# What is kept of the input projection: added by VectorE at every further visit instead of brought back to PSUM

## The chip, the cores and the metric

The program runs on one core of a Trainium2 chip. The metric is the device time of the whole program in microseconds (us); less is better. The engines named here are TensorE (PE, matmuls; PEld is its weight load), VectorE (DVE), ScalarE (ACT), GpSimd (POOL) and SyncE (SP, which issues the loads). Matmul results go to PSUM, which here is used in banks of 128 x 512 fp32.

## What is computed

Two residual layers over 256 tokens of width 2048. Only the first projection of the first layer matters for the change:

```
mod = (silu(c) @ ada_w[layer] + ada_b[layer])
sh_m, sc_m, g_m, sh_f, sc_f, g_f = split(mod, 6)
h = rmsnorm(x, norm_mix[layer]) * (1 + sc_m) + sh_m
z = h @ w_in                       # (256, 2048) @ (2048, 5632)
q, k, v, u, vg = split(z)          # 12 heads, 4 gating groups
...                                # rope(q), rope(k), attention, spatial gating, w_out, residual, FFN
```

Everything is fp32. Each weight matrix is used as a high part (fp32r) and a rest (fp32r), and so is `h`, so that one product takes three matmuls: high x high, high x low, low x high.

## The kernel before, in words

**Weights.** All weights are streamed in pieces of 128 x 1024 fp32 (512 KB), 8 slots deep (`raw`). ScalarE copies a piece to its high part (`hi_piece`, L557), VectorE subtracts it from the piece to get the rest (`lo_piece`, L902), in the same slot. Here both are called splits. Two pieces make a unit: 24 matmuls of 128 x 512 (L1345 to L1347), 12 for each half of the tokens (t = 0, 1). Every engine walks the same list of units: in its turn n it prepares the pieces of unit n+2, while TensorE works through the unit that it has reached. What an engine does within a turn is in order; turns of different engines are tied by semaphores alone.

**The projection's order.** The 11 column groups of `w_in` (512 columns each) need 16 row tiles of 128, in four quarters of `h`. The quarters of `h` become known late, since each needs a part of the modulation `mod`. So the groups are visited more than once. `VISITS` lists them: visits 0 to 10 take quarter 0 of all 11 groups, visits 11 to 28 take one more quarter each of the first six groups (18 visits of one unit), and visits 29 to 33 take three quarters at once of the other five. Visit v of 0 to 28 is unit v. Visit v accumulates in PSUM banks `acc_bank(v, t)`, which it shares with visit v-2; `freed` waits for the visit before to be out of a bank.

**What happens between visits.** After a first visit ScalarE copies the two banks to `kept` or `vtok` in SBUF (`evict`, L585). For the 18 visits in `SEEDED`, ScalarE copies what is kept back to PSUM ahead of the visit (`seed`, L591), TensorE waits for it (`begin`) and accumulates onto it with no start flag, and ScalarE copies the sum out again. For visits 29 to 33 VectorE adds PSUM to what is kept, in place (`add_visit`, L1136). In a turn n of VectorE this stands between the two splits; in a turn of ScalarE the copies stand around its second split.

**The modulation.** `ada_w` is streamed too, in the same SP queue. VectorE sums it row tile by row tile: one operation of 128 x 1024 for each (`ada_op`, L930), 16 for one result, at a pace written out by hand in `ADA_PACE`: turns 9 to 20 have 32 of them (2 or 3 a turn), turns 21 to 59 have 66 (1 or 2 a turn). They stand at the end of VectorE's turn. In `REDUCE_AT` (turns 9, 15, 21) TensorE, after its unit, turns two tiles of the normalized x and then reduces the finished result over the partitions (`reduce_cols`, L1395, 16 records). It waits for the last sum, which stands at the end of VectorE's turn 8, 14 and 20. VectorE then adds the bias (`keep_cols`, L948), and ScalarE and VectorE make the next quarter of `h`. SP issues the load of sum number a only after sum a-6 is done, and the pieces that follow it in the queue wait with it.

**After it.** GpSimd applies rope to q and k after the last visit of a group (`whole`), from turn 23 on. Turns 28 to 46 hold the attention, whose scores VectorE reads at the head of its turn.

Of the kernel before, what the change touches and what calls it, by code (L numbers as in the profile page):

```python
# [53 lines left out]
VISITS = ([(c, (0,)) for c in IN_ORDER]  # L54
          + [(c, (k,)) for k in (1, 2, 3) for c in IN_ORDER[:EARLY]]
          + [(c, (1, 2, 3)) for c in IN_ORDER[EARLY:]])
# [3 lines left out]
VISIT_AT = {u: v for v, u in UNIT_OF.items()}  # L60
BEFORE = {v: w for v, (c, ks) in enumerate(VISITS) for w in range(v) if VISITS[w][0] == c}

SEEDED = [v for v in BEFORE if len(VISITS[v][1]) == 1]
KEPT = {c: n for n, c in enumerate((0, 3, 1, 4, 2, 5, 9, 10))}
FIRST_OF = {k: min(u for u, x in enumerate(IN_UNITS) if x[2] == k) for k in range(4)}

# [10 lines left out]
G_F0 = G_OUT + 4  # L77
SEEDED += [G_F0 + n for n in range(2 * F_VISITED, len(F_UNITS))]
G_CI = G_F0 + 30 + 6 * F_VISITED
# [154 lines left out]
def acc_bank(g, t):  # L234
    return 2 * (g % 2) + t
# [6 lines left out]
def decoder_kernel(nc, x_in, c_col, pos, ada_w, ada_b, g_mix, g_ffn, w_in, sgu_w, sgu_b, w_out,  # L242
                   conv_in, conv_w, conv_out, ff_gate, ff_up, ff_down, g_fin, freq_in, ident_in,
                   mask_in, out):
    with ExitStack() as ctx:
# [148 lines left out]
        def kept_of(c, t):  # L394
            return kept[:, KEPT[c], t, :] if c in KEPT else vtok[:, t, COLS * (c - 6):COLS * (c - 5)]
# [156 lines left out]
        def _(sa):  # L552
# [30 lines left out]
            def evict(dst, g, t, func=ACT.Copy):  # L583
                sa.wait_ge(acc_done[t], g + 1)
                nc.scalar.activation(dst, ps[:, acc_bank(g, t), :], func).then_inc(acc_free[acc_bank(g, t)], 1)  # L585

            def seed(src, g, t, before):

                freed(sa, before, t)
                freed(sa, g - 2, t)  # L590
                nc.scalar.activation(ps[:, acc_bank(g, t), :], src, ACT.Copy).then_inc(seeded, 1)  # L591
# [62 lines left out]
            def keep_visit(v, t):  # L654

                if v not in BEFORE or v in SEEDED:
                    evict(kept_of(VISITS[v][0], t), v, t)
                if v + 2 < G_OUT and v + 2 in SEEDED:
                    seed(kept_of(VISITS[v + 2][0], t), v + 2, t, BEFORE[v + 2])
# [239 lines left out]
        def _(ve):  # L899
# [5 lines left out]
            def lo_next(u, half):  # L905
                if half:
                    row_low_part(u)
                if 2 * (u + 2) + half < PIECES:
                    lo_piece(2 * (u + 2) + half)
# [220 lines left out]
            def add_visit(v):  # L1130

                for t in range(2):
                    of = kept_of(VISITS[v][0], t)
                    ve.wait_ge(acc_done[t], v + 1)
                    freed(ve, BEFORE[v], t)
                    nc.vector.tensor_tensor(of, ps[:, acc_bank(v, t), :], of, ALU.add).then_inc(acc_free[acc_bank(v, t)], 1)  # L1136
# [40 lines left out]
            for n in range(46):  # L1177
# [16 lines left out]
                lo_next(n, 0)  # L1194
                if VISIT_AT.get(n) in BEFORE and VISIT_AT[n] not in SEEDED:
                    add_visit(VISIT_AT[n])
# [135 lines left out]
        def _(pe):  # L1332
            def half_unit(u, g, t, first, last, of, k0, half):

                v = 2 * u + half
                on = g in SEEDED
                to = ps[:, acc_bank(g, t), :]
# [15 lines left out]
            def begin(g, t):  # L1353
                if g in SEEDED:
                    pe.wait_ge(seeded, 2 * SEEDED.index(g) + t + 1)
                elif g >= 2:
                    freed(pe, g - 2, t)
# [354 lines left out]
```

## Time and profile before

| | |
|---|---|
| time, median of 3 runs | 2292.36 us (2292.32 to 2294.68) |
| profiled execution: its own time | 2291.94 us |
| its span, first to last instruction | 2290.2 us |
| busy: PE, DVE, ACT, POOL | 2226.5 us (97%), 1629.8 us (71%), 1132.7 us (49%), 104.3 us (5%) |
| DMA, mean | 269 GB/s |
| chain that ended last | PE 95%, DVE 3%, DMA 1%, issue 1%, ACT 1% |

The time of a run holds the span and 1.7 us around it. Busy shares are means over the whole span; the change touches the first tenth of it. The chain is followed back from the last instruction; "issue" in it is time in which an engine waited for nothing that the profile shows. The granted clock is given as a share of 2.4 GHz, so 0.50 is 1.2 GHz.

### The profile page before, as it was taken

To read this page: it belongs to the slowest core of one execution; us is meant where nothing else is said; L and a number is where in the kernel's file an instruction comes from. 1 tells how busy PE (TensorE), PEld (TensorE's weight loads), DVE (VectorE), ACT (ScalarE), POOL (GpSimd) and SP (SyncE) were. 2 spreads that over 40 slices of the span, in tenths; PEclk is the share of its full clock that TensorE was granted. 3 is DMA by queue.
4 is the path that set the end of the run, shared out by engine and by line. 5 is a ranking of instruction groups with operands and counts; after the bars stand their busy time and mean duration, and the time that the engine had idled before them with its cause. 6 is when DMAs were issued, how large, how long until landed. Compare 5 with 4: busy or idle time off the path is not lost.

```text
span 2290.2 us, 26677 instructions
## 1 busy us (share of the span) xinstructions
PE 2226.5 (97%) x10108; PEld 1844.7 (81%) x10108; DVE 1629.8 (71%) x1652; ACT 1132.7 (49%) x1496; POOL 104.3 (5%) x71
## 2 busy tenths in 40 slices
PE   3999999999999999999999999999999999999998
PEld 2877888788888888888878888887888888888887
DVE  5888988878877777777788777878644455445455
ACT  4677664578644334434464444446444343344443
POOL 0003201000000010000100000010000010000010
PEclk9999999999999999999999999999999999999999
DMA  9999889998888888888878888888766666666664
GB/s 338 353 351 346 277 276 307 320 341 306 300 307 287 300 297 306 287 296 288 303 262 285 301 287 294 285 285 284 239 192 188 190 192 193 193 187 191 192 190 141
DMA packets 286031, 615.89 MB, mean 269 GB/s; under 512 B 19792, under 2 KB 20176, under 8 KB 285520
## 3 DMA queue, kind: packets, MB, share of 16 engines
q1 hardware_dynamic: 284464, 613.50, 80.0%
q8 instruction: 80, 1.31, 0.2%
q10 hardware_dynamic: 1440, 0.69, 0.1%
q14 instruction: 47, 0.39, 0.0%
HBM read 612.02 MB, written 2.10 MB: 268 GB/s over the span
## 4 chain that ended last, share of the span: by engine, by line
PE 95%; DVE 3%; DMA 1%; issue 1%; ACT 1%; ACTq 0%; SPq 0%; DVEq 0%
PE ps L1345 30%; PE ps L1347 30%; PE ps L1346 30%; PE ps L1426 2%; DVE acc L930 1%; DMA ada<-ada_w 1%; PE ps L1395 1%; DVE wlo L902 1%; ACT hf L631 0%; DVE hf L1010 0%; DVE h L997 0%; DVE h L999 0%; PE ps L1568 0%; PE ps L1524 0%; PE ps L1410 0%
## 5 line engine op out<-in xcount | busy, mean ns | idle before, releaser
L902 DVE TENSOR_TENSOR wlo<-raw,whi 128x1024 fp32r<-128x1024 f32 x776 | 935.9, 1233 | 295.8 <-ACT whi L557 294.7
L557 ACT ACTIVATE whi<-raw 128x1024 fp32r<-128x1024 f32 x776 | 805.9, 1058 | 639.3 <-PE ps L1347 541.3
L1345 PE MATMUL ps<-whi,h 128*128 128x512 f32 x2144 | 844.6, 394 | 13.7 <-DVE h L999 8.3
L1347 PE MATMUL ps<-whi,h 128*128 128x512 f32 x2144 | 837.2, 390 | 0.0
L1346 PE MATMUL ps<-wlo,h 128*128 128x512 f32 x2144 | 836.8, 390 | 0.0
L930 DVE SCALAR_TENSOR_TENSOR acc<-ada,cact,acc 128x1024 f32<-128x1024 f32 x368 | 483.7, 1314 | 20.6 <-DMA ada<-ada_w 8.9
L1345 PEld LDWEIGHTS ps<-whi,h 128*128 128x128 f32 x2144 | 404.1, 188 | 101.2 <-DVE h L999 11.4
L1347 PEld LDWEIGHTS ps<-whi,h 128*128 128x128 f32 x2144 | 403.6, 188 | 85.3
L1346 PEld LDWEIGHTS ps<-wlo,h 128*128 128x128 f32 x2144 | 404.1, 189 | 82.1
L1345 PE MATMUL ps<-whi,act 128*128 128x512 f32 x704 | 275.0, 391 | 0.0
L1347 PE MATMUL ps<-whi,act 128*128 128x512 f32 x704 | 274.0, 389 | 0.0
L1346 PE MATMUL ps<-wlo,act 128*128 128x512 f32 x704 | 274.0, 389 | 0.0
L530 POOL TENSOR_TENSOR x<-x,tmp 128x512 f32<-128x512 f32 x40 | 70.0, 1751 | 1913.5 <-DVE tmp L1056 1912.3
L1347 PEld LDWEIGHTS ps<-whi,act 128*128 128x128 f32 x704 | 132.1, 188 | 27.5
L1345 PEld LDWEIGHTS ps<-whi,act 128*128 128x128 f32 x704 | 132.2, 188 | 27.2
L1346 PEld LDWEIGHTS ps<-wlo,act 128*128 128x128 f32 x704 | 132.2, 188 | 27.1
L1345 PE MATMUL ps<-whi,mixed 128*128 128x512 f32 x256 | 100.5, 393 | 0.0
L1347 PE MATMUL ps<-whi,mixed 128*128 128x512 f32 x256 | 99.7, 390 | 0.0
L1346 PE MATMUL ps<-wlo,mixed 128*128 128x512 f32 x256 | 99.7, 389 | 0.0
L1056 DVE TENSOR_TENSOR tmp<-ps,grow 128x512 f32<-128x512 f32 x48 | 33.2, 691 | 90.2 <-PE ps L1347 90.1
L1100 DVE TENSOR_TENSOR prod<-ps,silu 128x512 f32<-128x512 f32 x44 | 30.0, 690 | 80.5 <-PE ps L1347 80.5
L585 ACT ACTIVATE silu<-ps 128x512 f32<-128x512 f32 x44 | 26.2, 599 | 114.8 <-PE ps L1347 114.8
(131 smaller groups left out, 960.8 us busy)
## 6 DMA issues: line engine op xcount, KB each, us to landing
ada<-ada_w SPq DMA_DIRECT2D x384, 512.0 KB, 5.9
raw<-ff_gate SPq DMA_DIRECT2D x176, 512.0 KB, 3.8
raw<-ff_up SPq DMA_DIRECT2D x176, 512.0 KB, 3.8
raw<-ff_down SPq DMA_DIRECT2D x176, 512.0 KB, 4.2
raw<-conv_in SPq DMA_DIRECT2D x96, 512.0 KB, 4.0
raw<-w_in SPq DMA_DIRECT2D x88, 512.0 KB, 5.8
raw<-w_out SPq DMA_DIRECT2D x32, 512.0 KB, 5.9
raw<-conv_out SPq DMA_DIRECT2D x32, 512.0 KB, 4.8
```

The lines of the kernel that those rows point to most:

```text
L530: nc.gpsimd.tensor_tensor(xs, xs, tmp[:, r % 2, :], ALU.add).then_inc(x_pool, 1)
L557: nc.scalar.activation(whi[v % HIGH][:, :, :], raw[:, v % RAW], ACT.Copy).then_inc(hi_ready, 1)
L585: nc.scalar.activation(dst, ps[:, acc_bank(g, t), :], func).then_inc(acc_free[acc_bank(g, t)], 1)
L902: nc.vector.tensor_tensor(wlo[:, v % RAW], raw[:, v % RAW], whi[v % HIGH][:, :, :].bitcast(F32), ALU.subtract).then_inc(lo_ready, 1)
L930: nc.vector.scalar_tensor_tensor(out=to, in0=src, scalar=c, in1=to, op0=ALU.mult, op1=ALU.add)\
L1056: nc.vector.tensor_tensor(tmp[:, r % 2, :], ps[:, acc_bank(g, t), :], grow[:, COLS * n:COLS * n + COLS], ALU.mult).then_inc(acc_free[acc_b ...
L1100: nc.vector.tensor_tensor(prod[:, t, :], ps[:, acc_bank(g, t), :], silu[:, t, :], ALU.mult).then_inc(acc_free[acc_bank(g, t)], 1)
L1345: nc.tensor.matmul(to, high, whi[v % HIGH][:, k, :], start=begin, stop=False, skip_group_check=on)
L1346: nc.tensor.matmul(to, high, wlo[:, v % RAW, k, :], start=False, stop=False, skip_group_check=on)
L1347: ins = nc.tensor.matmul(to, low, whi[v % HIGH][:, k, :], start=False, stop=end, skip_group_check=on)
L1395: ins = nc.tensor.matmul(ps[:, ADA_BANK, COLS - 8 + n:COLS - 7 + n], sums[:, P * n:P * n + P], ones_r[:, 0:1].bitcast(F32), start=True, st ...
L1426: return nc.tensor.transpose(to, src, ident[:, :])
```

## The change

```
 BEFORE = {v: w for v, (c, ks) in enumerate(VISITS) for w in range(v) if VISITS[w][0] == c}

-SEEDED = [v for v in BEFORE if len(VISITS[v][1]) == 1]
+SEEDED = []
 KEPT = {c: n for n, c in enumerate((0, 3, 1, 4, 2, 5, 9, 10))}
```

`SEEDED` later also gets the visits of the first FFN, and those stay. For the 18 visits 11 to 28 the following changes, all through tests of `SEEDED`:

- ScalarE's `keep_visit` neither copies what is kept to PSUM nor copies the sum out (36 + 36 copies of 128 x 512 less).
- VectorE's turns 11 to 28 run `add_visit(v)`: two additions of 128 x 512, from PSUM and what is kept to what is kept, between the two splits. Each waits for the visit's matmuls and frees the bank.
- TensorE begins each of these visits with a start flag, and waits for the bank to be freed instead of for the seed.
- GpSimd's rope and the attention wait, through `freed`, for VectorE's addition instead of ScalarE's copy.

No load changes, and nothing moves in the SP queue.

## Rows read from the trace of the kernel before

**Rows 1.** Chain that ended last: start and length of pieces (us).
```profile
100.28 1.68 PE ps L1395 x16
...
135.77 4.15 issue
139.92 3.54 PE ps L1395 x16
...
148.79 0.29 PE ps L1345
...
179.67 1.79 issue
181.46 2.21 PE ps L1395 x16
183.67 0.64 PE ps L1345
...
186.44 0.24 PE ps L1345
```

**Rows 2.** VectorE in order of time: start, duration, operation [idle before, releaser].
```profile
111.04 1.22 DVE L902 TENSOR_TENSOR wlo<-raw,whi 128x1024 fp32r<-128x1024 f32 x1 [0.93 <-ACT whi L557]
112.18 4.05 DVE L930 SCALAR_TENSOR_TENSOR acc<-ada,cact,acc 128x1024 f32<-128x1024 f32 x3
...
135.76 4.06 DVE L930 SCALAR_TENSOR_TENSOR acc<-ada,cact,acc 128x1024 f32<-128x1024 f32 x3
139.74 2.35 DVE L902 TENSOR_TENSOR wlo<-raw,whi 128x1024 fp32r<-128x1024 f32 x2
143.50 0.17 DVE L948 TENSOR_TENSOR mod<-ps,adab 128x8 f32<-128x8 f32 x1 [1.41 <-PE ps L1395]
...
152.58 1.23 DVE L902 TENSOR_TENSOR wlo<-raw,whi 128x1024 fp32r<-128x1024 f32 x1 [1.58 <-ACT whi L557]
153.72 4.05 DVE L930 SCALAR_TENSOR_TENSOR acc<-ada,cact,acc 128x1024 f32<-128x1024 f32 x3
...
181.28 2.35 DVE L902 TENSOR_TENSOR wlo<-raw,whi 128x1024 fp32r<-128x1024 f32 x2
```

**Rows 3.** Stretches: length, busy time of each engine, granted clock, DMA share, GB/s.
```profile
130.00:134.00 4.00, 4.00 (x19) 3.34 (x18) 3.79 (x4) 3.54 (x6) 0.00 (x0) 1.00 1.05 386
...
140.00:142.00 2.00, 2.00 (x10) 2.00 (x11) 2.00 (x2) 0.59 (x1) 0.00 (x0) 0.50 1.06 389
```

**Rows 4.** ScalarE in order of time, a seed and the next split.
```profile
109.42 0.60 ACT L591 ACTIVATE ps<-kept 128x512 f32<-128x512 f32 x1
109.96 1.04 ACT L557 ACTIVATE whi<-raw 128x1024 fp32r<-128x1024 f32 x1
```

**Rows 5.** VectorE in order of time, around additions that exist already.
```profile
245.98 1.28 DVE L1136 TENSOR_TENSOR kept<-ps,kept 128x512 f32<-128x512 f32 x2
247.18 1.21 DVE L902 TENSOR_TENSOR wlo<-raw,whi 128x1024 fp32r<-128x1024 f32 x1
```

**Rows 6.** Chain that ended last, ends of units 26 to 29.
```profile
212.34 0.44 PE ps L1426 x4
...
218.27 0.44 PE ps L1426 x4
...
232.53 0.43 PE ps L1568 x2
```

**Rows 7.** VectorE in order of time, last sum of turn 27, start of turn 28.
```profile
220.64 1.76 DVE L930 SCALAR_TENSOR_TENSOR acc<-ada,cact,acc 128x1024 f32<-128x1024 f32 x1
226.42 0.56 DVE L1187 SCALAR_TENSOR_TENSOR prob<-ps,mask 128x384 f32<-128x384 f32 x1 [4.02 <-PE ps L1568]
...
227.73 2.35 DVE L902 TENSOR_TENSOR wlo<-raw,whi 128x1024 fp32r<-128x1024 f32 x2
```

**Rows 8.** Waits between 186 and 232 us: total, times, longest.
```profile
DVE wlo L902 <- ACT whi L557: 2.1, 4, 1.0
```

## The prediction

> **What bounds the kernel now.** I read the page's chain, then the chain in order of time, then VectorE's and ScalarE's order of time, then the stretches with their clock and the waits. The page's chain gives TensorE 95% of the span, so only what keeps TensorE from its matmuls, or adds to them, can count. The change lies in turns 9 to 28, about 96 to 232 us. The chain over this stretch [rows 1] is TensorE alone but for two holes: "issue" of 4.15 us from 135.77 and of 1.79 us from 179.67. Each ends in the reduction of a modulation result. What they wait for is seen in VectorE's order of time [rows 2]: the three sums from 135.76 end at 139.82, and the reduction starts at 139.92; the splits that follow the last sums start at 181.28, and the reduction starts at 181.46. So in both holes TensorE waits for the sixteenth sum, and VectorE is the engine that sets it. From 112.18 to the row of 139.74 the view has ten rows of VectorE and none shows idle time; from 153.72 to 181.28 ten more, again none. VectorE, 71% busy on the mean, is full in just these two stretches. ScalarE is not: it waits for pieces in them.
>
> A hole also lowers the clock. Around the first one the granted clock is 0.50 (1.2 GHz) [rows 3], and the reduction takes 3.54 us where it took 1.68 in turn 9 [rows 1]. Matmuls run at the low level until 148.79, 8.9 us after work resumed at 139.92; at half speed that is 4.4 us lost. After the second hole the reduction takes 2.21 (0.5 lost) and the low level lasts from 183.67 to 186.44 (2.8 us, 1.4 lost): 1.9 us lost.
>
> **The change, part by part.**
>
> *ScalarE.* From one seed to the next split is 109.96 - 109.42 = 0.54 us [rows 4], so 36 seeds and about as much for each of 36 copies out are some 40 us of ScalarE's time. It counts only where VectorE waits for a split of ScalarE's. In turn 10 VectorE does, 0.93 us, ahead of 111.04 [rows 2]. The seed of visit 12 (0.54) stands ahead of that split; with it gone and the copy out of visit 10 handing over a little sooner I take 0.7 us, bounds 0.54 and 0.93. So VectorE enters its full stretch 0.7 us earlier.
>
> *VectorE, first stretch.* Two additions take 1.28 us, but the next split starts 1.20 us after their start (247.18 - 245.98) [rows 5], so a visit costs 1.20 us where VectorE is full. The sixteenth sum of the second result stands at the end of turn 14. Ahead of it are the additions of turns 11, 12, 13, 14: 4 x 1.20 = 4.8 us, less 0.7: the sum comes 4.1 us later, bounds 3.8 and 4.8 (full 4 x 1.28 = 5.1, nothing won; less 0.93 on the other side). Nothing covers it, since TensorE stands idle at the end of that stretch already. The hole grows from 4.15 to 8.2 us. That bank v is free only after VectorE's addition, so that units 14 and 15 may start some tenths later, falls into the same hole.
>
> *Turns 15 and 16.* The addition of turn 15 lies between two splits while TensorE reduces, where VectorE idled 1.41 us ahead of 143.50 [rows 2]: 1.20 fits. In turn 16 VectorE idled 1.58 us ahead of 152.58 for ScalarE; the additions must await unit 16, end just there, and I take them at nothing, with 1.2 us as the upper bound. If either cover were gone it would be 1.2 us on the next hole.
>
> *VectorE, second stretch.* The sixteenth sum of the third result stands at the end of turn 20. Ahead of it in a full VectorE are the additions of turns 17 to 20: 4 x 1.20 = 4.8, less 0.15 that turn 16 gives: 4.65 us later, bounds 4.5 and 6.3. The hole grows from 1.79 to 6.4 us.
>
> *The clock.* The first hole already had its low level over the whole reduction, so I take its loss as unchanged; the second hole, now longer than the first one was, should lose what the first one did: 4.4 instead of 1.9, so 2.5 us more. Bounds: the low level may end as soon as it did after the second hole (5.0 us after work resumed, 2.5 lost, so -1.9 at the first hole and +0.6 at the second), or last through the reduction and one whole unit (1.9 + the 5.5 us of a unit, 218.27 - 212.34 - 0.44 [rows 6]: 7.4 lost, +3.0 and +5.5). The Trainium skill ("TensorE: Matmul & The Clock Gate", section "Loop structure matters more than you think") says that TensorE drops to its low clock during a long wait between groups of matmuls, while an engine emptying PSUM beside running matmuls does not do that; the trace agrees with the first half (0.50 after the 4.15 us hole), and the second is not what this kernel has, because here the engine that empties PSUM is also the one awaited. By that rule the sum is the same.
>
> *Turns 22 to 28.* VectorE now does 1.20 us more in each turn, and also slower where GpSimd's rope runs beside it: a sum takes 1.76 us [rows 7] instead of a third of 4.05. Cover: VectorE idles 4.02 us ahead of 226.42 [rows 7], and 2.1 us in four waits for ScalarE's splits [rows 8]. I take these 6 us as used up first. Six additions (turns 22 to 27) are 7.2 us, the rope may add 0.3 us to each of four turns; 8.4 less 6.1 leaves VectorE 2.3 us later than TensorE in turn 28. What is late next is the bank of visit 28, which unit 30 needs: the scores' four small operations (227.73 - 226.42 = 1.3 us), one split (112.18 - 111.04 = 1.1) and one addition (0.6) from 226.42 + 2.3 come to 231.8, and unit 30 starts at 232.53 + 0.43 = 232.96 [rows 6]. One us is left, so I take nothing, with 3 us as the upper bound (all seven turns 0.6 us dearer than thought). The Trainium skill ("GPSIMD Engine Reference", section "Specifications") says that GpSimd contends with VectorE instructions that read two SBUF inputs; an addition reads one input from PSUM, so by it the four would cost 1.20 each and 2.2 us would be left instead of one. No row here has an addition beside rope.
>
> *Waits moved.* TensorE's start of a visit waits for VectorE instead of ScalarE; behind it nothing but its own matmuls. Rope of q group 0 waits for the addition of turn 23; the first turned tile is needed three units later. SP's loads of `ada_w` wait for sums 6 back, so they go out later together with the sums, and pieces behind them still land turns ahead. At the end of unit 28 TensorE's scores wait for ScalarE, which stands between two copies out of visit 28 there; without them I take 0.2 us less, bounds 0 and 0.5 (one copy, as the seed of [rows 4]).
>
> **Sum.** 4.1 + 4.65 + 2.5 - 0.2 = 11.05 us. Everything behind turn 28 is bound by TensorE and moves as a block. Against the profiled execution: 2291.94 + 11.05 = 2303.0; its time is 0.42 below the median of the runs, so against the median 2292.36 + 11.05 = **2303.4 us** (0.5% slower).
>
> **The rivals.**
>
> *VectorE's backlog reaches the banks (slower still).* For it: one us of slack in the account above, and rope beside it. Against it: the pure count leaves that one. Its point: more than 0.15 us beyond my price in each of turns 22 to 28. At 0.6 a turn it is 4.2 - 1.0 = 3.2 us more, and a late bank again in turns 29 and 30 about as much: 2307 to 2310.
>
> *The loads set the pace of the sums (no change).* For it: in the full stretch the DMA engines run at 386 GB/s with a share of 1.05 [rows 3], and if sums came as `ada_w` lands, additions would fit into waits. Against it: twenty rows of VectorE without idle time. It would need both holes to be load waits: 2292.4.
>
> *ScalarE sets the pace (faster).* For it: VectorE waits for ScalarE's split ahead of 111.04 and 152.58 [rows 2], and ScalarE loses 40 us of work. It decides if ScalarE's relief brings VectorE forward by more than the 1.20 us of a visit. Then the holes close: 4.15 + 1.79 and their clock loss 4.4 + 1.9 are 12.2 us, so 2280. Against it: between 112.18 and 139.74 no row of VectorE waits for anything, so there is nothing to bring forward.
>
> That the change does nothing is no rival: the additions and the missing seeds follow from the list alone.
>
> **How the numbers follow.** The forecast has 0.72, with its own range of 2300 to 2306.5 (clock -1.3 to +3 and the small bounds). The backlog has 0.14, no change 0.07, faster 0.06, and 0.01 is left. The range from 2298 to 2309 reaches over most of the backlog's case and to a return of the clock at its earliest. About 0.2% (4.6 us) is what a measurement of this kernel can tell from no change. Slower by more: the forecast and the backlog, 0.86; a forecast so wrong in size that it lies within 4.6 us is counted with no change, 0.08; faster 0.06.
>
> **What the profile would show.** Right: in VectorE's order of time, L1136 with 46 additions in all and no L591 before the FFN; rows without idle time in the same two stretches, longer by 4 x 1.2 us each; "issue" of about 8.2 and 6.4 us in the chain ahead of L1395; both reductions at 3.5 us. Wrong: holes grown by less than 3 us each (then VectorE wasn't the pace), a low level of under 5 us after the second hole, TensorE waiting for VectorE's L1136 in units 24 to 30 (backlog), or waits of VectorE for loads in the full stretches.

## The result, and the profile after

The changed kernel takes 2302.59 us (median of 6 runs, 2301.59 to 2304.20) against 2292.73 us (6 runs, 2292.32 to 2294.68): 9.9 us more. The ratio is 1.0039, with a 95% interval of 1.0029 to 1.0049. The forecast was 2303.4 us.

The profiled execution took 2303.71 us with a span of 2302.0 us, 11.8 us above that of before. The chain that ended last, in order of time, answers to [rows 1] (start, length, what):

```profile
101.50 1.70 PE ps L1395 x16
...
131.29 0.69 DVE vtok L1136
132.02 0.50 PE ps L1345
...
138.64 6.58 issue
145.21 3.56 PE ps L1395 x16
...
184.52 6.55 issue
191.07 3.55 PE ps L1395 x16
...
199.09 0.42 PE ps L1346
```

Both holes are there and larger: 6.58 us where it was 4.15, 6.55 us where it was 1.79. The first row is the reduction of turn 9, which began at 100.28 before. So 1.22 us of the 11.8 were lost ahead of the change: in this execution the low clock at the very start lasted to 48.95 us instead of 46.15. Counted from reduction to reduction, the changed kernel needs 145.21 - 101.50 = 43.71 us (before 39.64, so +4.07) and 191.07 - 145.21 = 45.86 us (before 41.54, so +4.32). From the third reduction to the four matmuls at the end of unit 26 it is 224.24 - 191.07 = 33.17 us (before 30.88, +2.29). From there to the last matmuls of the scores behind unit 29 the changed kernel is 0.15 us shorter (244.28 - 224.24 = 20.04, before 232.53 - 212.34 = 20.19), and behind that nothing more is lost. 1.22 + 4.07 + 4.32 + 2.29 - 0.15 = 11.75 us, against 11.8. The rows of 131.29 and 132.02 show TensorE starting unit 15 when VectorE's first addition of visit 13 is done: the bank comes back from VectorE now. The longest of these waits is the one ahead of unit 14 (waits between 96 and 250 us: total, times, longest):

```profile
PE ps L1345 <- DVE kept L1136: 0.9, 1, 0.9
```

VectorE in order of time answers to [rows 2], [rows 5] and [rows 7] (start, duration, operation, idle time before):

```profile
111.54 1.23 DVE L902 TENSOR_TENSOR wlo<-raw,whi 128x1024 fp32r<-128x1024 f32 x1 [0.20 <-ACT whi L557]
112.68 4.06 DVE L930 SCALAR_TENSOR_TENSOR acc<-ada,cact,acc 128x1024 f32<-128x1024 f32 x3
...
117.80 1.28 DVE L1136 TENSOR_TENSOR kept<-ps,kept 128x512 f32<-128x512 f32 x2
...
141.05 4.06 DVE L930 SCALAR_TENSOR_TENSOR acc<-ada,cact,acc 128x1024 f32<-128x1024 f32 x3
...
146.16 1.28 DVE L1136 TENSOR_TENSOR kept<-ps,kept 128x512 f32<-128x512 f32 x2
...
148.79 0.17 DVE L948 TENSOR_TENSOR mod<-ps,adab 128x8 f32<-128x8 f32 x1 [0.22 <-PE ps L1395]
...
155.07 1.22 DVE L902 TENSOR_TENSOR wlo<-raw,whi 128x1024 fp32r<-128x1024 f32 x1 [0.87 <-ACT whi L557]
156.21 1.28 DVE L1136 TENSOR_TENSOR vtok<-ps,vtok 128x512 f32<-128x512 f32 x2
157.41 1.22 DVE L902 TENSOR_TENSOR wlo<-raw,whi 128x1024 fp32r<-128x1024 f32 x1
158.54 4.06 DVE L930 SCALAR_TENSOR_TENSOR acc<-ada,cact,acc 128x1024 f32<-128x1024 f32 x3
...
186.92 4.05 DVE L930 SCALAR_TENSOR_TENSOR acc<-ada,cact,acc 128x1024 f32<-128x1024 f32 x3
...
218.81 1.48 DVE L902 TENSOR_TENSOR wlo<-raw,whi 128x1024 fp32r<-128x1024 f32 x1
220.21 1.28 DVE L1136 TENSOR_TENSOR vtok<-ps,vtok 128x512 f32<-128x512 f32 x2
...
238.19 0.56 DVE L1187 SCALAR_TENSOR_TENSOR prob<-ps,mask 128x384 f32<-128x384 f32 x1 [1.03 <-PE ps L1568]
```

The addition pairs stand between the splits, each 1.28 us long and 1.20 from its start to the next split. The sixteenth sum of the second result ends at 141.05 + 4.06 = 145.11, and the reduction starts at 145.21. Ahead of 111.54 VectorE idles 0.20 us where it idled 0.93. In turn 16 (155.07 to 158.54) the addition stands in what was idle time. Of the 4.02 us ahead of the first scores 1.03 are left (238.19). And the addition at 220.21 ran beside rope in its usual 1.28, while the split ahead of it took 1.48.

The stretches that show the clock (columns as in [rows 3]), first in and behind the first hole, then in and behind the second:

```profile
142.00:144.00 2.00, 0.00 (x0) 0.00 (x0) 1.79 (x3) 0.00 (x0) 0.00 (x0) 0.50 1.04 383
...
150.00:152.00 2.00, 2.00 (x7) 1.58 (x6) 1.78 (x2) 1.97 (x6) 0.00 (x0) 0.60 1.05 400
```

```profile
186.00:188.00 2.00, 0.00 (x0) 0.00 (x0) 2.00 (x2) 0.00 (x0) 0.00 (x0) 1.00 1.01 376
...
198.00:200.00 2.00, 2.00 (x7) 1.58 (x6) 0.71 (x2) 1.97 (x4) 0.00 (x0) 0.66 0.00 0
```

At the first hole the clock was low in the last part of it and back at 151.5 us, 6.3 after work resumed (the last matmul of the low level ends there). At the second it was still full until 188 us, 3.5 us into the hole, fell, and came back at 199.5 us, 8.4 after work resumed.

### The profile page after: what moved, and what is told of

It is laid out like the page before. It is cut to its first block, busy times and chain, and to the rows that moved or that the text cites. A ratio compares the mean times of both kernels' runs of the same rounds, so it can differ in the third digit from the quotient of the medians.

```text
span 2302.0 us, 26641 instructions
## 1 busy us (share of the span) xinstructions
PE 2229.8 (97%) x10108; PEld 1846.9 (80%) x10108; DVE 1649.5 (72%) x1688; ACT 1093.6 (48%) x1424; POOL 103.8 (5%) x71
## 4 chain that ended last, share of the span: by engine, by line
PE 92%; DVE 4%; issue 2%; DMA 1%; ACT 1%; ACTq 0%; SPq 0%; DVEq 0%
PE ps L1345 29%; PE ps L1347 29%; PE ps L1346 29%; PE ps L1426 2%; DVE acc L930 2%; PE ps L1395 1%; DMA ada<-ada_w 1%; DVE wlo L902 1%; ACT hf L631 1%; DMA raw<-w_in 0%; ACT whi L557 0%; DVE hf L1010 0%; DVE h L997 0%; DVE h L999 0%; PE ps L1568 0%
```

## Experiments

All times are medians beside runs of the kernel before on the same chip, whose median was 2293.5, 2293.6 and 2293.2 us in the three groups. "R1, R2, R3" are the starts of the reductions of turns 9, 15 and 21 in the profiled execution; before R1 to R2 is 39.64 us and R2 to R3 is 41.54 us. R5 is the fifth reduction, counted from R1, far behind the change (at 446.85 us before). "The stage" is the time from R1 to R5: 346.6 us before, 357.1 us in the changed kernel, +10.5.

The stage is given because a total can hold something else. From R5 to the end, where none of the edits reaches, the profiled execution took 1843.3 to 1843.5 us before, in the changed kernel and in e1, e3, e4, f1, f2 and f3, but 1845.0 to 1845.4 us in e2, e5, e6, e7, e8 and g1: in those six the clock fell once more, in the second layer (shown at e7). How often this happens in their other executions is not on record.

### Which additions cost: e1 to e3

One line chooses the visits that stay seeded:

```diff
-SEEDED = []
+SEEDED = [v for v in BEFORE if len(VISITS[v][1]) == 1 and v in (11, 12, 13, 14, 17, 18, 19, 20)]   # e1
+SEEDED = [v for v in BEFORE if len(VISITS[v][1]) == 1 and v in (15, 16, 21, ..., 28)]              # e2
+SEEDED = [v for v in BEFORE if len(VISITS[v][1]) == 1 and v in (15, 16, 17, ..., 28)]              # e3
```

> Seeds stay for visits 11 to 14 and 17 to 20, whose additions would stand ahead of a sixteenth sum in a full VectorE; the other ten visits (15, 16, 21 to 28) are added by VectorE. My theory (an addition costs only where VectorE is full ahead of a sum that TensorE awaits): same time as the kernel before, 2290.5 to 2294.5 us, with holes of about 4.2 and 1.8 us ahead of the reductions. Rival (each addition costs its share wherever it stands, by PSUM banks that come free late or by work beside rope): 10/18 of the 10 us, so about 2298 us.

Measured: 2296.49 us, ratio 1.0014 (1.0005 to 1.0024), 3 us above before. R1 to R2 is 39.64 us, as before, but R2 to R3 is 43.16; the stage is 2.9 us longer. Neither the theory (no loss) nor the rival (5 us) holds.

> The complement: only visits 11 to 14 and 17 to 20 are added by VectorE, the other ten are seeded as before. Theory: the whole loss of the changed kernel, 2301 to 2304 us, with both holes at 6.3 to 7 us and both reductions at about 3.5 us. Rival (each addition costs its share): 8/18 of the 10 us, about 2297 us.

Measured: 2309.20 us, ratio 1.0068 (1.0056 to 1.0081), 15.7 us above before: 6 us worse than the changed kernel, which has ten additions more. Both missed it. In the profiled execution the stage is 15.9 us longer than before, and another 1.6 us are lost far behind. The chain shows holes of 8.2 us:

```profile
138.33 8.17 issue
...
186.62 8.18 issue
```

> Only visits 11 to 14 are added by VectorE. Theory: the first hole grows by 4 us (in the changed kernel 6.6 us were left, since units 14 and 15 began late as well), the second stays at about 1.8 us with its short low clock; the time is 3.5 to 4.5 us above before, 2296 to 2297.5 us. Rival (the loads catch up over the hole, so that VectorE's loss in the first stretch is given back in the second): under 2 us above before.

Measured: 2300.59 us, ratio 1.0030 (1.0019 to 1.0042), 7.1 us above before (the stage +6.6). R1 to R2 is 46.08 us, 2.4 more than with all visits added, and R2 to R3 is 41.78, so nothing was given back. The reason for the excess is in two views of this run. ScalarE in order of time:

```profile
130.66 0.60 ACT L591 ACTIVATE ps<-kept 128x512 f32<-128x512 f32 x1 [7.68 <-DVE vtok L1136]
131.19 1.04 ACT L557 ACTIVATE whi<-raw 128x1024 fp32r<-128x1024 f32 x1
```

and VectorE:

```profile
129.88 1.28 DVE L1136 TENSOR_TENSOR vtok<-ps,vtok 128x512 f32<-128x512 f32 x2
132.27 1.23 DVE L902 TENSOR_TENSOR wlo<-raw,whi 128x1024 fp32r<-128x1024 f32 x1 [1.11 <-ACT whi L557]
...
138.52 1.28 DVE L1136 TENSOR_TENSOR kept<-ps,kept 128x512 f32<-128x512 f32 x2
140.90 1.22 DVE L902 TENSOR_TENSOR wlo<-raw,whi 128x1024 fp32r<-128x1024 f32 x1 [1.10 <-ACT whi L557]
```

A seed of visit v+2 copies to the bank of visit v. Where visit v is added, the seed waits for VectorE's addition; ScalarE's second split stands behind the seed, and VectorE's second split waits for that: 1.1 us of idle time ahead of 132.27 and of 140.90. It happens in each turn in which an addition is followed by a seed: turns 13 and 14 in e3 (2 x 1.1 of the 2.4 us), 15 and 16 in e1, and 13, 14, 19, 20 in e2. In the changed kernel no seed is left, so it has none of it. This was a new theory, tested by f1 to f3.

### The relief of ScalarE: e4

```diff
+                if 11 <= v <= 28:
+                    sa.wait_ge(acc_done[t], v + 1)
+                    fill_once()              # a copy of 128 x 512 to a tile that nobody reads
+                if 11 <= v + 2 <= 28:
+                    fill_once()
```

> The changed kernel, but ScalarE does 72 copies of 128 x 512 that nobody needs, where its seeds and its copies out of visits 11 to 28 stood, half of them behind the same wait for the visit's matmuls. Theory (ScalarE was no pace, its relief brought 0.7 us at turn 10 and 0.5 us at turn 16): 0.5 to 2 us above the changed kernel, 2303 to 2304.6 us. Rival (the relief of 40 us of ScalarE's work has hidden part of what the additions cost): 4 us or more above the changed kernel, over 2306.5 us.

Measured: 2303.66 us, ratio 1.0044 (1.0031 to 1.0057), 1.1 us above the changed kernel. With its 72 copies back ScalarE is as busy as before (66.2 us between 96 and 196 us; before 65.6 us between 96 and 186; changed kernel 39.5), and the time hardly moves; the stage is 357.0 us, as without them. ScalarE was no pace.

### Seeds behind additions: f1 to f3

f1 adds only visits 21 to 28, so no seed follows an addition. f2 is e1 and f3 is e2, with ScalarE's second split ahead of the seeds in the turns concerned:

```diff
                 hi_next(n, 0)
+                handed = v in BEFORE and v not in SEEDED and v + 2 in SEEDED
+                if handed:
+                    hi_next(n, 1)
                 for t in range(2):
                     if v is not None:
                         keep_visit(v, t)
-                    if t == 0:
+                    if t == 0 and not handed:
                         hi_next(n, 1)
```

> Visits 11 to 20 are seeded as before, only the last eight (21 to 28) are added by VectorE, so no seed follows an addition. Theory (the additions of turns 21 to 28 are covered, and what the run with ten additions lost came from seeds behind additions): the time of the kernel before within 1.5 us, holes of 4.2 and 1.8 us. Rival (VectorE's backlog in turns 22 to 28 costs 2 us or more by itself): 2 to 4 us above before.

Measured: 2293.41 us, ratio 1.0000 (0.9991 to 1.0009). The additions of turns 21 to 28 cost nothing that the medians tell from zero.

> The run with ten additions (visits 15, 16, 21 to 28) again, but in the two turns in which an addition is followed by a seed, ScalarE does its second split ahead of the seeds. Theory (there ScalarE's seed waited for VectorE's addition and VectorE's second split waited for ScalarE's, 1.1 us of idle time of VectorE in each such turn): no idle time of VectorE ahead of those splits, second hole back to about 1.8 to 2.5 us, 1.5 to 3 us faster than with the seeds first, 2293 to 2295 us. Rival (the seeds' order is harmless, the two additions cost by themselves): no change against the run with ten additions.

Measured: 2291.77 us, ratio 0.9996 (0.9987 to 1.0005), 4.7 us below e1, more than expected. R2 to R3 is 41.0 us instead of 43.2, and the stage is 2.0 us shorter than in e1; where the rest of the 4.7 comes from the two profiled executions don't show. Ten of the 18 visits can be added without loss.

> The run with the eight additions of the full turns again, with ScalarE's second split ahead of the seeds in turns 13, 14, 19 and 20. Theory (four handovers of 1.1 us fall away, the additions' own 1.2 us a turn stay): 4 to 5.5 us faster than with the seeds first, 2303 to 2305.5 us, which is the changed kernel's time: those eight additions are all of its loss. Rival: still over 2307 us.

Measured: 2301.96 us, ratio 1.0038 (1.0025 to 1.0050), 7.2 us below e2, again more than expected, and the changed kernel's time. The stage is 6.2 us shorter than in e2; 1.6 us of e2's excess was the clock far behind. The chain:

```profile
138.21 5.86 issue
144.07 3.54 PE ps L1398 x16
...
183.53 5.83 issue
189.37 3.55 PE ps L1398 x16
```

R1 to R2 is 43.69 us, R2 to R3 45.30 (changed kernel: 43.71 and 45.86). So the eight additions in the full turns are all of the loss.

### How much cover the late additions had: e7

```diff
+                    if v in (22, 23, 24, 25, 26, 27, 28):
+                        if spares:
+                            ve.wait_ge(spared, len(spares))
+                        spares.append(0)
+                        nc.vector.tensor_tensor(spare[:, :], ps[:, acc_bank(v, t), :], x[:, t, 0:COLS], ALU.add).then_inc(spared, 1)
                     nc.vector.tensor_tensor(of, ps[:, acc_bank(v, t), :], of, ALU.add)...
```

> The changed kernel with a second VectorE operation of 128 x 512 from PSUM ahead of each addition of visits 22 to 28 (14 more, 1.2 us a turn, 8.4 us in all, result unused). It measures the slack that the additions of these turns had. Theory (VectorE idled 1.0 us ahead of the first scores, and an addition of visit 28 had about 2 to 3 us before unit 30 needs its bank): TensorE loses 8.4 - 1.0 - 2.5 = about 4 to 6 us, 2306.5 to 2309 us. Rival (there is slack of more than 8 us, the backlog that the prediction feared was far off): within 1.5 us of the changed kernel, under 2304.1 us.

Measured: 2309.94 us, ratio 1.0072 (1.0059 to 1.0084), 7.35 us above the changed kernel for 8.4 us of work. But not all of that was lost where the additions stand. R5 in the chain of the changed kernel, and then of e7:

```profile
458.59 1.68 PE ps L1395 x16
```

```profile
463.39 1.68 PE ps L1403 x16
```

From R3 (191.07 and 190.55) to R5 is 267.5 and 272.8 us: 5.3 us more, within the 4 to 6 expected. So 8.4 - 5.3 = 3.1 us of the work was covered, and not only the 1.03 us of idle time ahead of the first scores. TensorE waits for VectorE's additions for 2.8 us between 96 and 250 us in this run (1.5 in the changed kernel). The other 2.0 us are in the stretch behind R5 (1845.4 against 1843.4 us). There, in the second layer, TensorE waits for a split: 2.05 us until 1585.39 in the changed kernel, 2.40 us until 1590.57 in e7. Behind that wait the clock stays full in the one and is low in the other (columns as in [rows 3]):

```profile
1586.00:1588.00 2.00, 2.00 (x10) 1.61 (x9) 2.00 (x3) 0.82 (x1) 0.00 (x0) 1.00 0.95 376
```

```profile
1592.00:1594.00 2.00, 2.00 (x6) 1.58 (x5) 2.00 (x3) 0.00 (x0) 0.00 (x0) 0.50 0.34 133
```

The five other runs named above have the same wait (2.04 or 2.05 us), and there too the clock falls; in the kernel before it is 2.04 us, and there the clock stays full.

### The hole itself: e5, e6, e8, g1

If the loss is TensorE waiting for a late sum, TensorE may do other work first. e5 (kernel before) and e6 (changed kernel) reduce after unit 16 and 22 instead of ahead of them; e8 (kernel before) reduces between their two pieces:

```diff
                     norm_turn(0, 2 * REDUCE_AT[n] + 1)
-                    reduce_cols(REDUCE_AT[n])
+                    if n == 9:
+                        reduce_cols(REDUCE_AT[n])
+                if n - 1 in (15, 21):                 # e5, e6: in TensorE's loop, behind unit(n, ...)
+                    reduce_cols(REDUCE_AT[n - 1])
...
+                    if half == 0 and u - 1 in (15, 21):   # e8, g1 instead: in unit(), behind the first piece
+                        reduce_cols(REDUCE_AT[u - 1])
```

> The kernel before, but TensorE runs the second and third reduction after its unit 16 and 22 instead of ahead of them; nothing else moves. Theory: the unit fills the hole in which TensorE waited for the sixteenth sum, so the chain ahead of the reduction has no hole and the reduction runs at the full clock (1.7 us); what is lost is that unit 17 and 23 then wait for their quarter of h, about 3.5 us after each reduction. First place: unit 17 starts some 4 to 5 us earlier than before, second: 0 to 1 us. 2286.5 to 2289 us. Rival (the quarter of h comes late enough that the wait only changes its place): within 2 us of before.

Measured: 2292.85 us, ratio 0.9998 (0.9989 to 1.0007), no change: the rival, by the total. The chain:

```profile
142.14 1.68 PE ps L1395 x16
143.82 3.48 issue
147.30 0.77 PE ps L1345
...
182.85 1.68 PE ps L1395 x16
184.53 3.56 issue
```

The reductions take 1.68 us and no hole is ahead of them, but 3.48 and 3.56 us of waiting for the quarter of h stand behind, and eight matmuls at 0.43 us behind each. The waits changed their place, and their effect on the clock went with them, which the expectation had left out. The stage is 1.3 us shorter than before, and the stretch far behind 1.7 us longer.

> The same move in the changed kernel. Theory: the sums come 4 us later in each stretch, so a hole of about 1.2 us stays ahead of the first reduction and of about 1.2 us ahead of the second, the clock stays high, and both waits for the quarter of h follow: 2290 to 2295 us, about what the kernel before needs. If the low clock were no part of the loss, it would gain less than 5.4 us at each place and stay above 2296 us.

Measured: 2301.28 us, ratio 1.0034 (1.0021 to 1.0046), 1.3 us below the changed kernel, far from the 2290 to 2295 expected (the stage is 2.7 us shorter, the stretch far behind 1.6 longer). Ahead of the third reduction there is no hole any more, but VectorE gets to its part of the result no sooner:

```profile
190.37 1.28 DVE L1136 TENSOR_TENSOR kept<-ps,kept 128x512 f32<-128x512 f32 x2
191.57 1.22 DVE L902 TENSOR_TENSOR wlo<-raw,whi 128x1024 fp32r<-128x1024 f32 x1
192.70 0.16 DVE L948 TENSOR_TENSOR mod<-ps,adab 128x8 f32<-128x8 f32 x1
```

The reduction was done at 191.33. The bias addition (L948) runs at 192.70, behind the addition of visit 21 and the second split, without idle time. In this kernel VectorE's whole list of work up to L948 is the pace, not only the sums. What TensorE does in the hole changes little. It does not settle what the low clock costs: behind the reductions TensorE waits up to 4.9 us for its quarter of h, and the clock falls there.

> The kernel before, with the second and third reduction between the two pieces of unit 16 and 22 (half a unit, 2.7 us, of matmuls ahead of them, half behind). Theory: of the first hole 1.4 us are left, of the second none, the clock stays high, and the second half of the unit covers 2.7 of the 3.5 us until the quarter of h is there: 5 to 6.5 us faster at the first place and 2 to 3 us at the second, 2284 to 2287 us, faster than both kernels and than the move by a whole unit. Rival (VectorE, not TensorE, sets the second sum anyway, so what is won at the first place is lost at the second): 2288 us or more.

Measured: 2289.64 us, ratio 0.9983 (0.9974 to 0.9992), 3.9 us faster than before and faster than both kernels. TensorE's waits between 96 and 250 us (total, times, longest), then VectorE's order of time:

```profile
PE ps L1397 <- issue: 2.8, 2, 1.4
PE ps L1345 <- issue: 0.8, 1, 0.8
...
```

```profile
136.43 4.06 DVE L930 SCALAR_TENSOR_TENSOR acc<-ada,cact,acc 128x1024 f32<-128x1024 f32 x3
140.41 2.35 DVE L902 TENSOR_TENSOR wlo<-raw,whi 128x1024 fp32r<-128x1024 f32 x2
142.68 0.16 DVE L948 TENSOR_TENSOR mod<-ps,adab 128x8 f32<-128x8 f32 x1
```

Two holes of 1.4 us are left ahead of the reductions. The bias addition at 142.68 follows VectorE's splits with no idle time, where it idled 1.41 us in [rows 2]. Behind the first reduction seven matmuls still run at 0.43 us, behind the second none. The stage is 4.7 us shorter than before, where 7 to 9.5 us were expected: the gain ends where VectorE's own list becomes the pace. Another 1.7 us of the miss is the clock far behind.

g1 is e8 with the sums of turns 14 and 20 ahead of VectorE's second split:

```diff
+                if n in (14, 20):
+                    ada_ops(n)
                 lo_next(n, 1)
...
-                ada_ops(n)
+                if n not in (14, 20):
+                    ada_ops(n)
```

> The kernel before with both reductions between the pieces of unit 16 and 22, and in turns 14 and 20 VectorE does its sums ahead of its second split, so that the sixteenth sum comes 1.1 us sooner. Theory (VectorE's chain of sums sets both places): holes of about 0.3 us instead of 1.4, the clock stays high behind the reduction (1.6 us at each place in the run with the split first), 2 to 5 us faster than that run, 2284.5 to 2288 us. Rival (the second split is then late for unit 16 and 22, or the quarter of h is the pace): no faster than 2289 us.

Measured: 2289.09 us, ratio 0.9981 (0.9972 to 0.9990): 0.5 us below e8 by the medians, which the intervals don't tell apart; the stage is the same (341.8 us in both). VectorE:

```profile
135.57 4.06 DVE L930 SCALAR_TENSOR_TENSOR acc<-ada,cact,acc 128x1024 f32<-128x1024 f32 x3
139.55 3.49 DVE L902 TENSOR_TENSOR wlo<-raw,whi 128x1024 fp32r<-128x1024 f32 x3
142.95 0.16 DVE L948 TENSOR_TENSOR mod<-ps,adab 128x8 f32<-128x8 f32 x1
```

Counted from R1 (101.21 here, 100.94 in e8), the sixteenth sum is done 1.1 us sooner, but three splits in a row now stand ahead of the bias addition, which starts 41.74 us after R1 in both. The theory (the sums are the pace) fell once more, for the reason seen in e6: the split that was moved was only moved within the list that has to be done.

## Why the prediction was right

**VectorE's additions ahead of a sixteenth sum are the loss: right, shown by f1 and f3.** With those eight alone the time is 2301.96 us, with only the last eight of the others it is 2293.41.

**First stretch, 4.1 us:** 4.07 measured from R1 to R2. That is 4.8 less 0.73; the idle time ahead of 111.54 fell by just that. The hole was foretold as 8.2 us and is 6.58. The sum is the same: 1.65 us of it was lost earlier, most of it where units 14 and 15 waited 0.90 and 0.31 us for their bank, which the prediction called "some tenths".

**Turns 15 and 16 at nothing:** right. VectorE's idle time ahead of L948 fell from 1.41 to 0.22 us, and turn 16 even became shorter, from 153.72 - 149.78 = 3.94 to 158.54 - 155.07 = 3.47 us.

**Second stretch, 4.65 us:** 4.32 measured. The 0.15 taken for turn 16 was 0.47.

**The clock, +2.5 us at the second hole:** the reduction took 3.55 instead of 2.21 us, and unit 22 ran low until 199.5; together 2.29. At the first hole the low level ended 6.3 us after work resumed, not 8.9. It changed little, because VectorE and not TensorE set the next reduction; the prediction's bound of -1.9 us for an early return had counted TensorE's time there as passed on in full. That the clock's share is right in size is read from one execution of each kernel, and it is partly luck: how long the low level lasts differs between executions with the same wait. In f1 TensorE waits 2.08 us ahead of R3, hardly more than the 1.79 before, but the reduction takes 3.44 us instead of 2.21, and from R3 to R5 it is 1.5 us longer than before (266.9 against 265.4). So the low clock costs by itself, apart from the length of the hole; no run took the hole away and left the low clock.

**Turns 22 to 28 at nothing, one us left:** the price was right, as f1 shows; the account behind it was not. It had VectorE 2.3 us behind TensorE in turn 28, but VectorE still idles 1.03 us ahead of the first scores (238.19), and e7 shows 3.1 us of cover, not one. The term that was wrong is the rope, taken as 0.3 us more in each of four turns. Summed over the splits and sums of turns 22 to 27, what they take above their usual 1.22 and 1.28 us beside rope fell from 4.4 us before to 2.7. From VectorE's last operation on h (188.42 before, 199.36 after) to the end of turn 27's sums its work, idle time left out, grew from 31.9 to 37.2 us: 5.3 us for six additions of 1.20, not 8.4. The error was on the safe side and left the price at nothing. "GPSIMD Engine Reference", section "Specifications", of the Trainium skill says that GpSimd contends with VectorE instructions of two SBUF inputs; the trace agrees: the addition at 220.21 kept its 1.28 us beside rope, the split at 218.81 took 1.48. That the additions now fill part of the time beside rope, where a split or a sum would have been slowed, would explain the fall; no run tests it.

**The small term, -0.2 us at the first scores:** -0.15 measured up to the scores behind unit 29.

**The rivals.** The loads as the pace: VectorE has no idle time in the full stretches, and each addition shows in full. ScalarE as the pace: excluded by e4. The backlog: not reached; e7 puts it some 3 us of further work away.

**What the prediction did not see** was no part of it: that a seed behind an addition costs 1.1 us of VectorE's time a turn (e1 to e3), and that the clock can fall once more far behind the change (e7).

## What to carry to other kernels

Price an operation by what stands behind it in its engine's list, up to the next thing that the bound engine awaits, not by how busy the engine is on the mean: the same 1.20 us was lost in full in eight turns and cost nothing in ten. Where two engines pass buffers to each other in order, work that depends on the other engine belongs behind the work that the other engine awaits (1.1 us a turn here). And a small dependent step on the bound engine can go between two pieces of independent work, which shortened the two holes here from 4.15 and 1.79 to 1.4 us each and gained 3.9 us in all, but only until the waiting engine's own list is the pace; then moving things within that list gains nothing. Last, compare runs over the stage that was changed as well as by their totals: in six runs here 1.6 to 2.0 us of the total arose over 1300 us behind the change.

## What the hardware showed that was not expected

- The low clock lasted for very different times after work resumed: 5.0 us (before, second hole of 1.79 us), 8.9 us (before, first hole, 4.15), 6.3 and 8.4 us (after, holes of 6.58 and 6.55). The length of the hole doesn't order them.
- A short wait can lower the clock or leave it: TensorE's wait of 2.0 to 2.1 us in the second layer left it full in the profiled executions of before, the changed kernel and f1 and lowered it in those of e2, e5, e6, e8 and g1, which cost 1.6 to 1.7 us each time.
- The start of the program alone varies by over 1 us between two executions (the turn-9 reduction at 100.28 and at 101.50), through the moment at which the clock rises (46.15 and 48.95 us).
- ScalarE's plain copy of 128 x 512 from SBUF to PSUM (0.60 us) is only some 0.08 us shorter than VectorE's addition of the same size (0.68 us), which reads two inputs. And VectorE starts its next instruction some 0.1 us before the end that the record gives (1.28 us for a pair of additions, 1.20 to the next start).
